# A two-block transformer kernel: the order of loads and the work before the first product

## The reference

```
mod = silu(c) @ w_ada + b_ada            # shift, scale, gate: 1024 numbers each
h   = rms_norm(x, norm_g) * (1 + scale) + shift
(a.., b.., c.., d..) = split(h @ w_in)   # queries, keys, values, z of four branches
x   = x + gate * (merged @ w_out)        # merged: the four branches, gated
```

## Time and profile before

| | |
|---|---|
| median of 3 runs | 1125.09 us |
| lowest to highest | 1125.05 to 1125.93 us |
| the profiled execution | 1125.82 us |
| its span | 1124.5 us |
| TensorE busy | 97% of the span |
| VectorE, ScalarE, GpSimd busy | 67%, 49%, 4% |
| first product of the first quarter (L961) starts | 20.50 us |
| first product after the four quarters (L659) starts | 55.87 us |

### The profile page before, as it was taken

One profiled execution on the slowest core, in us unless ns is written; L12 is line 12 of the kernel. 1 busy time (PEld: TensorE's weight loads), 2 busy tenths in 40 slices (PEclk: granted clock), 3 DMA queues, 4 the chain that ended last, 5 costly groups with the idle time before them and its releaser, 6 DMA issues.

```text
span 1124.5 us, 15034 instructions
## 1 busy us (share of the span) xinstructions
PE 1094.6 (97%) x6141; PEld 947.2 (84%) x6141; DVE 759.0 (67%) x1049; ACT 548.0 (49%) x782; POOL 49.2 (4%) x82
## 2 busy tenths in 40 slices
PE   3999999999999999999999999999999999999997
PEld 3689988787888888988988988788988989888986
DVE  4637676865779998655687855556977546788743
ACT  2347654444451346555444444456765546444442
POOL 3021000000010000000100000000011000000000
PEclk9999999999999999999999999999999999999999
DMA  9965454755656404534665565554444436555450
GB/s 347 330 198 168 131 188 135 276 188 169 224 150 174 150 1 147 198 122 133 169 206 189 180 215 172 185 186 151 141 159 152 149 112 206 183 192 188 150 187 38
DMA packets 118358, 195.08 MB, mean 173 GB/s; under 512 B 6297, under 2 KB 39217, under 8 KB 118288
## 3 DMA queue, kind: packets, MB, share of 16 engines
q1 hardware_dynamic: 115728, 187.51, 50.2%
q0 software_dynamic: 2560, 6.60, 2.0%
HBM read 193.04 MB, written 1.05 MB: 173 GB/s over the span
## 4 chain that ended last, share of the span: by engine, by line
PE 90%; DVE 4%; ACT 3%; DMA 1%; issue 1%; POOL 1%; SPq 0%; ACTq 0%; DVEq 0%; POOLq 0%
PE product L659 55%; PE product L696 5%; PE small L696 5%; PE product L2473 5%; PE product L698 3%; PE small L698 3%; PE small L2497 2%; PE product L961 2%; ACT w_high L583 1%; PE small L806 1%; PE small L2038 1%; DMA w_raw<-in_w_ada 1%; PE small L721 1%; DVE w_low L593 1%; PE small L1408 1%
## 5 line engine op out<-in xcount | busy, mean ns | idle before, releaser
L593 DVE TENSOR_TENSOR w_low<-w_raw,w_high 128x2048 fp32r<-128x2048 f32 (+3 forms) x160 | 349.9, 2190 | 174.3 <-ACT w_high L583 172.7
L583 ACT ACTIVATE w_high<-w_raw 128x2048 fp32r<-128x2048 f32 (+3 forms) x160 | 292.1, 1832 | 177.2 <-PE product L659 145.5
L659 PE MATMUL product<-w_high,H 128*128 128x512 f32 (+2 forms) x736 | 239.5, 393 | 0.1
L659 PEld LDWEIGHTS product<-w_high,H 128*128 128x128 f32 x736 | 137.9, 188 | 28.5 <-issue 2.2
L659 PE MATMUL product<-H,w_high 128*128 128x256 f32 x816 | 150.4, 282 | 0.2 <-ACT queries_keys L1055 0.2
L659 PE MATMUL product<-w_low,H 128*128 128x512 f32 (+2 forms) x368 | 142.3, 387 | 0.0
L659 PEld LDWEIGHTS product<-H,w_high 128*128 128x128 f32 x816 | 126.5, 188 | 2.2 <-issue 1.3
L659 PE MATMUL product<-H,w_low 128*128 128x256 f32 x408 | 114.2, 280 | 0.0
L696 PE MATMUL product<-H,w_high 128*128 128x512 f32 x256 | 89.1, 391 | 0.0
L696 PE MATMUL small<-H,w_high 128*128 128x512 f32 x256 | 89.1, 391 | 0.0
L659 PEld LDWEIGHTS product<-w_low,H 128*128 128x128 f32 x368 | 69.3, 188 | 11.7 <-issue 0.2
(11 more groups left out here) (395 smaller groups left out, 1733.6 us busy)
## 6 DMA issues: line engine op xcount, KB each, us to landing
w_raw<-in_ffn_w_gate SPq DMA_DIRECT2D x20, 1024.0 KB, 5.0
w_raw<-in_ffn_w_up SPq DMA_DIRECT2D x20, 1024.0 KB, 5.0
w_raw<-in_ffn_w_down SPq DMA_DIRECT2D x20, 1024.0 KB, 4.9
w_raw<-in_w_merge SPq DMA_DIRECT2D x16, 1024.0 KB, 5.0
w_raw<-in_w_ada SPq DMA_DIRECT2D x16, 512.0 KB, 8.9
w_raw<-in_mem_w_k SPq DMA_DIRECT2D x8, 1024.0 KB, 4.9
w_raw<-in_mem_w_v SPq DMA_DIRECT2D x8, 1024.0 KB, 5.0
w_raw<-in_conv_w_pw SPq DMA_DIRECT2D x16, 512.0 KB, 4.8
```

Of the source, the lines that this page charges most:

```text
L583: k.act.eng.activation(parts_of(k, i, j)[0], raw_of(k, i), ACT.Copy).then_inc(*k.act.tells("weights_high", ("weights high", i)))
L593: k.vec.eng.tensor_tensor(low, raw, high.bitcast(F32), ALU.subtract).then_inc(*k.vec.tells("weights_low", ("weights low", i)))
L659: mm = pe.eng.matmul(bank[:, off:off + wide], a, r, start=b not in started, stop=True, skip_group_check=True)
```

## The change

- The constants are ordered anew and come in two transfers: 144 of 528 columns (the identity and the exponent -0.5) first, the rest ahead of ("whole", 0). The ones for the first three quarters' columns are part of the 528; `pe_first_columns` waits for the rest in the last quarter only, since ones and identity lie in different transfers and the event is implied before.
- Each chunk of w_ada for a quarter comes as two halves of two tiles of rows, each half as two transfers of 256 KB with an event of its own, and VectorE waits for a half before its two multiplications.
- X comes as two transfers, one for each tile of tokens, between w_ada (0,0) and (0,4), and ScalarE squares a tile when it has landed.
- A "whole" chunk's block of features is loaded in its place; its block of values is loaded after the next chunk, and TensorE waits for it before the values' items.
- The first quarter's x is not taken from `scaled_x`: ScalarE writes a diagonal matrix of roots for each tile of tokens, and TensorE multiplies x by it, which scales and turns at once. ScalarE scales all of X after the first quarter.
- TensorE multiplies a tile of zeros (written by VectorE) 5 times after the transpose of c and 7 times after the transpose of the condition's rows.
- On TensorE the next quarter's x is turned after the four feature items, not after the first, and its columns are computed one item later. In the first quarter x comes before the columns.
- VectorE takes the low part of the quarter before between a quarter's sums and its columns, not after the columns.

```diff
@@ -53,8 +53,8 @@
 W_D_Q, W_D_K, W_D_V, W_D_Z = 2700, 2956, 3212, 3468
 
 
-COMMON = {"ident": (0, 128), "ones": (128, 128), "causal": (256, 256), "invfreq": (512, 8), "half": (520, 8)}
-COMMON_W = 528
+COMMON = {"ident": (0, 128), "half": (128, 8), "ones": (136, 128), "causal": (264, 256), "invfreq": (520, 8)}
+COMMON_W, COMMON_FIRST = 528, 144
 FIRST = {"alibi": (0, 1024), "window": (1024, 1024), "decay": (2048, 1024), "strict": (3072, 384),
          "after": (3456, 128), "cmp_bias": (3584, 64), "cmp_mask": (3648, 64), "block": (3712, 256)}
 FIRST_W = 3968
...
@@ -425,7 +425,8 @@
         self.gate = self.sb("gate", [P, D])
         self.after_gate = self.at
         self.c_row, self.cond_rows, self.cond_cols = self.sb("c_row", [KT, P]), self.sb("cond_rows", [3 * KT, P]), self.sb("cond_cols", [P, 3 * KT])
-        self.scaled_x = self.sb("scaled_x", [P, NT, D])
+        self.scaled_x, self.first_diagonal = self.sb("scaled_x", [P, NT, D]), self.sb("first_diagonal", [P, NT, P])
+        self.zeros = self.HN[:, 1, 0:P + S]
         self.whole = self.HN[:, 0, :].rearrange("p (k n) -> p k n", n=S)
 
     def layout_branches(self):
@@ -599,8 +600,10 @@
 
     V, i = k.vec, k.whole_weights[name, n, first]
     raw, total = raw_of(k, i), modulation_sums(k, name, n)
-    V.wait_ge("c silu", ("weights", i), "gate bias" if name == "gate" else None)
+    V.wait_ge("c silu", *([("weights", i), "gate bias"] if name == "gate" else []))
     for j in range(CK):
+        if name != "gate":
+            V.wait_ge(("weights", i, j // 2))
         number = k.c_silu[:, first + j:first + j + 1]
         V.wait_ge(V.last)
         if first + j == 0 and name != "gate":
@@ -905,10 +908,21 @@
 
     key, sums = ("columns", q), modulation_sums(k, "first", q)
     bank = k.small.take(key)
-    k.pe.wait_ge(("first", q), "common", k.small.before(key))
+    k.pe.wait_ge(("first", q), "common rest" if q == QUARTERS - 1 else "common", k.small.before(key))
     for j in range(4):
         mm = k.pe.eng.matmul(bank[:, j:j + 1], sums[:, j * P:(j + 1) * P], k.ones[:, 0:1], start=j == 0, stop=True, skip_group_check=True)
     mm.then_inc(*k.pe.tells("columns", key))
+
+
+def pe_scale_and_turn_x(k):
+
+    bank = k.small.take(("x", 0))
+    k.pe.wait_ge("first diagonal", k.small.before(("x", 0)))
+    for j in range(2):
+        for t in range(NT):
+            at = j * S + t * P
+            mm = k.pe.eng.matmul(bank[:, at:at + P], k.X[:, t, j * P:(j + 1) * P], k.first_diagonal[:, t, :], start=at == 0, stop=True, skip_group_check=True)
+    mm.then_inc(*k.pe.tells("turned", ("x turned", 0)))
 
 
 def pe_turn_x(k, q):
@@ -921,14 +935,23 @@
     tr.then_inc(*k.pe.tells("turned", ("x turned", q)))
 
 
+def pe_warm(k, n):
+
+    k.pe.wait_ge("zeros")
+    for _ in range(n):
+        k.pe.eng.matmul(k.product.tensors[-1][:, 0:S], k.zeros[:, 0:P], k.zeros[:, P:P + S], start=True, stop=True, skip_group_check=True)
+
+
 def pe_condition(k):
     pe, tr = k.pe, k.pe.eng.transpose
     pe.wait_ge("common", "c row")
     tr(k.small.take("c")[:, 0:KT], k.c_row[:, :], k.ident[0:KT, 0:KT]).then_inc(*pe.tells("turned", "c turned"))
+    pe_warm(k, 5)
     pe.wait_ge("condition rows")
     tr(k.small.take("condition")[:, 0:3 * KT], k.cond_rows[:, :], k.ident[0:3 * KT, 0:3 * KT]).then_inc(*pe.tells("turned", "condition turned"))
+    pe_warm(k, 7)
+    pe_scale_and_turn_x(k)
     pe_first_columns(k, 0)
-    pe_turn_x(k, 0)
 
 
 def pe_first_block(k):
@@ -944,9 +967,11 @@
         x = k.whole[:, q % 2 * 2:q % 2 * 2 + 2, :]
         pe.wait_ge(("weights", k.split[i]), ("whole", q))
         for n, (name, b, off, t, col, w) in enumerate(items):
-            if q < QUARTERS - 1 and n == 1:
+            if n == CK:
+                pe.wait_ge(("weights", k.split[i], "values"))
+            if q < QUARTERS - 1 and n == CK:
                 pe_turn_x(k, q + 1)
-            if q < QUARTERS - 1 and n == CK:
+            if q < QUARTERS - 1 and n == CK + 1:
                 pe_first_columns(k, q + 1)
                 if q + 2 == QUARTERS:
                     pe.ended("condition")
@@ -984,12 +1009,17 @@
     A.eng.activation(k.c_silu, k.small.of("c")[:, 0:KT], ACT.Silu).then_inc(*A.tells("c_silu", "c silu", k.small.free("c")))
     sums = k.stat(("sums", "first"), NT)
     for t in range(NT):
-        A.wait_ge("x loaded")
+        A.wait_ge(("x loaded", t))
         A.eng.activation(k.scaled_x[:, t, :], k.X[:, t, :], ACT.Square, accum_out=sums[:, t:t + 1]).then_inc(*A.tells("squares", "first squares"))
     for t in range(NT):
-        A.wait_ge(A.last, ("root", "first"))
+        A.wait_ge(("root", "first"))
+        A.eng.activation(k.first_diagonal[:, t, :], k.ident, ACT.Copy, scale=k.stat(("root", "first"), NT)[:, t:t + 1]).then_inc(
+            *A.tells("first_diagonal", "first diagonal"))
+    act_first_quarter(k, 0)
+    for t in range(NT):
+        A.wait_ge(A.last)
         A.eng.activation(k.scaled_x[:, t, :], k.X[:, t, :], ACT.Copy, scale=k.stat(("root", "first"), NT)[:, t:t + 1]).then_inc(*A.tells("scaled_x", "scaled x"))
-    for q in range(QUARTERS):
+    for q in range(1, QUARTERS):
         act_first_quarter(k, q)
     act_split(k, QUARTERS)
     act_split(k, QUARTERS + 1)
@@ -1016,15 +1046,16 @@
 
 def vec_condition(k):
     V = k.vec
+    V.eng.memset(k.zeros, 0.0).then_inc(*V.tells("zeros", "zeros"))
     for q in range(QUARTERS):
-        for first in range(0, KT, CK):
-            vec_modulation(k, "first", q, first)
+        vec_modulation(k, "first", q, 0)
         if q == 0:
             V.wait_ge("condition turned")
             V.eng.tensor_copy(k.cond_cols[:, :], k.small.of("condition")[:, 0:3 * KT]).then_inc(*V.tells("cond_cols", k.small.free("condition")))
-        vec_first_columns(k, q)
+        vec_modulation(k, "first", q, CK)
         if q:
             vec_first_low(k, q - 1)
+        vec_first_columns(k, q)
     vec_split(k, QUARTERS)
     vec_first_low(k, QUARTERS - 1)
     vec_split(k, QUARTERS + 1)
@@ -3170,22 +3201,41 @@
 
 def sp_program(k):
     sp, w = k.sp, k.w
-    sp.eng.dma_start(k.common[:, :], w["common_constants"]).then_inc(*k.landed("load_common", "common"))
+    rest, x = slice(COMMON_FIRST, COMMON_W), w["x"][0].rearrange("(t p) n -> p t n", p=P)
+    sp.eng.dma_start(k.common[:, 0:COMMON_FIRST], w["common_constants"][:, 0:COMMON_FIRST]).then_inc(*k.landed("load_common", "common"))
     sp.eng.dma_start(k.c_row[:, :], w["c"][0].rearrange("(k p) -> k p", p=P)).then_inc(*k.landed("load_c", "c row"))
+    values = None
     for i, (pieces, _, into) in enumerate(k.plan):
-        at = 0
         if into == ("first", 0, CK):
-            sp.eng.dma_start(k.X[:, :, :], w["x"][0].rearrange("(t p) n -> p t n", p=P)).then_inc(*k.landed("load_x", "x loaded"))
+            for t in range(NT):
+                sp.eng.dma_start(k.X[:, t, :], x[:, t, :]).then_inc(*k.landed(f"load_x{t}", ("x loaded", t)))
+        if into == ("whole", 0):
+            sp.eng.dma_start(k.common[:, rest], w["common_constants"][:, rest]).then_inc(*k.landed("load_common_rest", "common rest"))
         if into[0] == "whole":
             n = k.split.index(i)
-            free, sem, slot = ("multiplied", n - k.N_SPLIT) if n >= k.N_SPLIT else None, f"load_first{n}", k.w_first[n % k.N_SPLIT]
+            slot = chunk_view(k, k.w_first[n % k.N_SPLIT], i)
+            sp.wait_ge(("multiplied", n - k.N_SPLIT) if n >= k.N_SPLIT else None)
+            sp.eng.dma_start(slot[:, :, 0:CN], pieces[0][0]).then_inc(*k.landed(f"load_first{n}", ("weights", i)))
+            values = i, n, slot[:, :, CN:2 * CN], pieces[1][0]
         else:
             n = k.raw_at[i]
-            free, sem, slot = ("weights low", k.in_raw[n - k.N_RAW]) if n >= k.N_RAW else None, f"load_w{n % k.N_RAW}", k.w_raw[n % k.N_RAW]
-        for src, n in pieces:
-            sp.wait_ge(free)
-            sp.eng.dma_start(chunk_view(k, slot, i)[:, :, at:at + n], src).then_inc(*k.landed(sem, ("weights", i)))
-            at += n
+            slot = chunk_view(k, k.w_raw[n % k.N_RAW], i)
+            sp.wait_ge(("weights low", k.in_raw[n - k.N_RAW]) if n >= k.N_RAW else None)
+            if into[0] == "first":
+                for half in range(2):
+                    tiles = slice(2 * half, 2 * half + 2)
+                    for b, (src, wide) in enumerate(pieces):
+                        sp.eng.dma_start(slot[:, tiles, b * wide:(b + 1) * wide], src[:, tiles, :]).then_inc(
+                            *k.landed(f"load_half{half}_{n % k.N_RAW}", ("weights", i, half)))
+            else:
+                at = 0
+                for src, wide in pieces:
+                    sp.eng.dma_start(slot[:, :, at:at + wide], src).then_inc(*k.landed(f"load_w{n % k.N_RAW}", ("weights", i)))
+                    at += wide
+            if values:
+                of, n, dst, src = values
+                sp.eng.dma_start(dst, src).then_inc(*k.landed(f"load_values{n}", ("weights", of, "values")))
+                values = None
```

(8 more changed lines are left out.)

## The result

The changed kernel takes 1127.88 us (median of 16 runs, 1125.95 to 1130.91), the kernel before 1125.05 us (16 runs beside them, 1124.01 to 1128.27). The ratio is 1.0025, 95% interval 1.0019 to 1.0032: slower by 2.8 us, where 4 us faster was forecast. The profiled execution took 1127.73 us, with a span of 1126.4.

What follows compares the result with a forecast made beforehand. TensorE, busy 97%, was taken as the bound, its start a matter of which bytes come first. 3.2 + 2.8 + 0.2 - 1.7 = 4.5 us gained, giving 1121.1 us; range 1119.2 to 1124.8.

Steps and rivals of the forecast that it cites:

- second assumption on the clock: At the start: TensorE's clock, once raised by zeros, stays up through gaps of 0.4 to 2, 0.7 and 1.7 us.
- First quarter's inputs and X: Before the first columns: w_ada's sums ready 1.9 us sooner, X's roots and diagonals ready at 13.0 us.
- Zeros: TensorE's start: twelve matmuls of zeros raise the clock to full pace, ending near 11 to 12.6 us, at no cost.
- rival (a): At the start: the clock does not rise on zeros; 1126.6 us, slower than before; chance 0.09.
- rival (b): At the start: the clock rises but falls again from 12.6 to 17.3 us, leaving 0.7 gain, 1125.1 us; chance 0.09.
- Gain 3.2 for the start: First quarter: TensorE's products start at 17.3 us instead of 20.5, a gain of 3.2 us.
- Gain 2.8 for the pace: First quarter: at full clock it takes 8.5 us instead of 11.3, a gain of 2.8 us.
- Gain 0.2 later: Later quarters: VectorE's low part no longer holds up TensorE, 0.1 us each, two times.
- Loss 1.7 at the heads: After the quarters: columns one item later delay ScalarE and VectorE, so TensorE waits for ScalarE's heads, losing 1.7 us.
- rival (d): At ScalarE's heads: they don't hold TensorE, the 1.7 us are not given back; 1119.6 us; chance 0.08.
- Halves: w_ada (0,4) in two halves: VectorE multiplies the first while the second lands, sums ready 1.9 us sooner.
- rule on large transfers: w_ada loads: at least 1 MiB per transfer; sixteen more cost 32 us by the page, taken as zero, 0.5 kept for range.

Runs made afterwards that it cites:

- fill_gap: The changed kernel with zeros in all of TensorE's early gaps and in its wait at ScalarE's heads: 1123.71 us, ratio 0.9992 to the kernel before.
- fill: The changed kernel with more matmuls of zeros, in all of TensorE's early gaps (15, 1 and 4): 1124.18 us, ratio 0.9995 to the kernel before.
- cols2: The changed kernel with the next quarter's columns one item earlier, in their old place, measured a second time on another chip: 1123.26 us, ratio 0.9981.
- gap: The changed kernel with 3 matmuls of zeros inside TensorE's wait at ScalarE's heads: 1125.79 us, ratio 1.0006 to the kernel before.
- cols: The changed kernel with the next quarter's columns one item earlier, in their old place: 1124.14 us, ratio 0.9991 to the kernel before.
- before_late: The kernel before with only the next quarter's columns moved one item later on TensorE: 1129.4 us, ratio 1.0037 to the kernel before.
- fill_gap_pieces: The changed kernel with zeros in early gaps and the heads' wait, each w_ada chunk in two 512 KB transfers again: 1123.48 us, ratio 0.9985.
- nozeros: The changed kernel without any matmul of zeros: 1128.05 us, ratio 1.0025 to the kernel before.
- best_hold: The changed kernel with early gaps zero-filled, columns one item earlier in second and third quarter, 4 more zero matmuls before the second quarter's columns: 1123.33 us, ratio 0.9983.
- fill_cols: The changed kernel with zeros in all early gaps and the next quarter's columns one item earlier: 1124.28 us, ratio 0.9998 to the kernel before.
- best: The changed kernel with zeros in all early gaps and columns one item earlier in the second and third quarter only: 1124.44 us, ratio 0.9993.
- before_fill: The kernel before with zeros in TensorE's early gaps (5, 18 and 3) and columns one item later in the first two quarters: 1124.21 us, ratio 0.999.

## Why the prediction was wrong

The part that failed is its second assumption on the clock, "I also take it that the clock stays up". It stands in the step on the zeros and went into two terms. The runs put these numbers to the steps:

- **First quarter's inputs and X** (x ready at 13.0): measured 14.4. The inputs came 0.8 to 0.9 us later than I said, in this execution; fill_gap's profile has the forecast times with the same loads, so this is not a wrong step but a spread that I had not allowed for. The sum of small steps on ScalarE and GpSimd was taken too short, by 0.5 us in the power alone.
- **Zeros.** The rise came, on zeros as on numbers; rival (a) fell. But the gaps that I listed, 0.4 to 2, 0.7 and 1.7 us, were 3.5, 0 and 1.8, and the fall came within the first (windows of 1 us show 1.00 up to 14 us and 0.50 from 14 on; TensorE is idle from 10.9 to 14.4). The evidence against rival (b), over 4 us at the end of the run, was one case, and I read it as a bound. Rival (b) is what happened, and `fill` shows it: with the gaps closed 3.7 us come back (I had priced it 3.8). Half pace cost 0.8 on the columns (1.71 against 0.95), 1.0 on x (2.07 against 1.05) and 2.2 on the quarter (10.6 against 8.4).
- **Gain 3.2 for the start**: 0.7 measured; 1.7 with the gaps filled (18.76).
- **Gain 2.8 for the pace**: 0.7 measured; 2.9 with the gaps filled (8.4 us). The 0.7 is one execution's: with the same start the first quarter took 9.9 us in cols2's profile and 11.5 in gap's.
- **Gain 0.2 later**: none; the quarters lie 8.42 apart, and 8.22 once the columns are back in their place (cols2).
- **Loss 1.7 at the heads**: right in place and size (1.71 us), so rival (d) fell. What I left out is that this idle time is itself paid twice. `gap` measures the second part at 2.1 us, `cols` and `before_late` the sum at 3.7 and 4.1. With this, rival (b)'s 1125.1 becomes 1127, near the measured 1127.9, and a sum that I had called positive on its own terms (0.7) turns negative. The range ended at 1124.8 because (b) was priced at a gain of 0.7 and given 0.09. From the forecast's 1121.1 the missing terms are 2.5 (start), 2.1 (pace), 0.2 (later) and 1.7 to 2.1 (the clock behind the heads), 6.5 to 6.9 in all; measured are 6.8 more.
- **Halves** (1.9 us on the sums): their effect on the sums is real in part (12.28 to 15.46 against 13.31 to 16.42), but `fill_gap_pieces` shows none on the time.

The Trainium skill's rule on large transfers (DMA: Bandwidth & Descriptors, Rules for kernel authors) was weighed the right way for the long stretch. In the first microseconds its direction can be seen: from 5 to 10 us the nine profiles with pieces of 256 KB move 343 to 357 GB/s, the four with pieces of 512 KB 361 to 392 (fill_gap_pieces 373). That is worth tenths of a microsecond, not 2 us a piece, and what causes it is not shown.

Three slips of the text on record: the columns that it calls the third quarter's are the last quarter's; the column of ones that TensorE multiplies by lies in the constants' first transfer, unlike what the list of changes says of it; and the chances of a faster time add up to 0.78, not 0.77.

Left open: why the clock fell near 200 us in some profiled executions (fill, gap, nozeros, before_late, best_hold) and not in others of nearly the same kernel. Of the four profiles with the full wait of 1.71 us at the heads only the changed kernel's shows the fall behind it; the other three (fill, nozeros, before_late) show one near 200 us. That the wait makes the clock fall rests on gap, on before_late and on the mean clocks of all executions, not on where single profiles show it. I did not try to hold TensorE busy near 200 us. Nor were the diagonal, the values' later load and the new order on VectorE tried by themselves.

## What to carry to other kernels

A wait of TensorE of a microsecond or two is not priced by its length alone: look at the granted clock of the windows behind it, and count the slower work too. Matmuls of zeros are worth something only if they reach up to the work they are for; here the ones that ended 3.5 us early brought nothing and the ones that closed the gaps brought 3.7 us. Before an operation is moved back on the busiest engine, ask which other engine's last work hangs on it; here one line cost more than all the rest of the change gained.

## What the hardware showed that was not expected

- The granted clock fell behind idle times of 1.5 to 1.8 us between dense matmuls (55 to 65 us in the changed kernel; behind 24.1 in fill_cols; behind 32.5 in best), while at the end of the run it took over 4 us. The same wait did not always bring the fall: in fill's profile, with 1.71 us before 52.86, windows of 50 to 70 show 1.00. How often it comes can't be read from single profiles. The mean clocks say: in nearly every execution of the changed kernel, but not in at least five of fill's eleven, which stand at 0.998 or 0.999. The medians agree: gap differs from the changed kernel by 2.1 us, fill_gap from fill by only 0.5. Why the two differ is not shown.
- Matmuls whose operands are all zero raise the clock and keep it up as others do: 36 records in 8.04 us (before_fill, from 8.27), each at full pace.
- The page prints 1.00 before the first recorded rise, where records run at half pace (10 of them in 4.44 us). At the very start the durations are to be trusted.
